# Another order of stages in a hybrid encoder step: the sample tile first, no stage behind its producer, no empty slots

## The reference

```
h = x + 0.5 * rms(SwiGLU_1(rms(x)))                    F1: 1024 -> 2 x 2816 -> 1024
z = rms(h) @ w_in                                      IP: 5376 columns: q | k | v | r,k,v,lora | gates
A = differential attention (4 heads, two softmax maps, rotary; prompt: block-causal, sample: 1024 cached keys + 16 own)
B = RWKV-7 mixing (8 heads of 64; each row's input is mixed with the row before it; a 64x64 state runs on)
m = sigmoid(gA) * (A @ w_o_att) + sigmoid(gB) * (B @ w_o_rwkv)
h = h + rms(m @ w_out)                                 OP
y = h + 0.5 * rms(SwiGLU_2(rms(h)))                    F2
```

## Time and profile before

| | us |
|---|---|
| median of 3 runs (3283.29 to 3289.14) | 3287.9 |
| time of the profiled execution | 3277.8 |
| its span | 3275.9 |
| PE busy | 3052.7 (93%) |
| DVE, ACT, POOL busy | 1732.7, 1263.5, 474.0 |
| mean granted TensorE clock | 0.968 of full |

### The profile page before, as it was taken

The page is one execution under the profiler, slowest core; times in us unless marked ns, Lnnn a source line. Parts: engine busy times, 40 slices in busy tenths (PEclk is TensorE's granted clock), DMA queues, the critical chain, the costliest instruction groups (busy, mean ns, idle before and its releaser), DMA issues.

```text
span 3275.9 us, 58322 instructions
## 1 busy us (share of the span) xinstructions
PE 3052.7 (93%) x23880; PEld 2701.3 (82%) x23880; DVE 1732.7 (53%) x2956; ACT 1263.5 (39%) x2494; POOL 474.0 (14%) x609
## 2 busy tenths in 40 slices
PE   7999999999999999989999899899889999996997
PEld 7998999789898877977779779787678788886996
DVE  4456445445556455376465555566555553454454
ACT  4334334344433343344344334333333332343432
POOL 0000000003022040220220310411411401200000
PEclk9999999999999999999999999999989998998998
DMA  5445444556334364564454433445644633463443
GB/s 153 126 127 175 133 129 142 188 177 205 94 118 136 117 217 140 154 204 153 137 156 130 141 103 95 140 152 195 200 140 141 194 124 111 144 210 126 126 129 112
DMA packets 499814, 482.78 MB, mean 147 GB/s; under 512 B 28563, under 2 KB 401708, under 8 KB 499534
## 3 DMA queue, kind: packets, MB, share of 16 engines
q1 hardware_dynamic: 472846, 389.16, 38.2%
q0 software_dynamic: 26704, 89.91, 8.6%
HBM read 431.77 MB, written 48.18 MB: 147 GB/s over the span
## 4 chain that ended last, share of the span: by engine, by line
PE 81%; DVE 7%; DMA 4%; issue 3%; ACT 2%; POOL 1%; SPq 0%; DVEq 0%; ACTq 0%; POOLq 0%
PE ps L252 41%; PE ps L262 25%; PE ps L978 4%; PE ps L1661 1%; DVE wlo L217 1%; PE ps L1677 1%; PE ps L1703 1%; DMA att<-out_dram 1%; DVE yb L884 1%; DMA att<-in_cache_att_v_dram 1%; ACT gB L826 1%; PE ps L983 1%; PE ps L970 1%; PE ps L1714 1%; DVE xnlo L539 1%
## 5 line engine op out<-in xcount | busy, mean ns | idle before, releaser
L217 DVE TENSOR_TENSOR wlo<-raw,whi 128x512 fp32r<-128x512 f32 x1140 | 823.8, 725 | 945.9 <-ACT whi L209 943.8
L209 ACT ACTIVATE whi<-raw 128x512 fp32r<-128x512 f32 x1140 | 712.8, 629 | 741.7 <-PE ps L252 389.0
L252 PE MATMUL ps<-xnhi,whi 128*128 128x384 f32 x2688 | 931.7, 347 | 18.9 <-issue 9.0
L252 PE MATMUL ps<-xnhi,wlo 128*128 128x384 f32 x2688 | 906.6, 337 | 0.0
L252 PE MATMUL ps<-xnlo,whi 128*128 128x384 f32 x2688 | 906.3, 337 | 0.0
L252 PEld LDWEIGHTS ps<-xnhi,whi 128*128 128x128 f32 x2688 | 510.4, 190 | 47.2 <-issue 27.7
L252 PEld LDWEIGHTS ps<-xnlo,whi 128*128 128x128 f32 x2688 | 510.8, 190 | 2.0 <-issue 1.7
L252 PEld LDWEIGHTS ps<-xnhi,wlo 128*128 128x128 f32 x2688 | 510.0, 190 | 0.0
L262 PE MATMUL ps<-whi,hidhi 128*128 128x512 f32 x936 | 384.7, 411 | 8.9 <-DVE yb L585 4.1
L262 PE MATMUL ps<-wlo,hidhi 128*128 128x512 f32 x936 | 369.3, 395 | 0.0
L262 PE MATMUL ps<-whi,hidlo 128*128 128x512 f32 x936 | 369.1, 394 | 0.0
(11 more groups left out here) (294 smaller groups left out, 3252.1 us busy)
## 6 DMA issues: line engine op xcount, KB each, us to landing
raw<-in_ffn_w_in_dram SPq DMA_DIRECT2D x528, 256.0 KB, 2.9
raw<-in_ffn_w_out_dram SPq DMA_DIRECT2D x264, 256.0 KB, 2.6
raw<-in_w_in_dram SPq DMA_DIRECT2D x252, 256.0 KB, 2.8
xt<-h_scratch SPq DMA_DIRECT2D x36, 512.0 KB, 5.5
att<-in_cache_att_k_dram POOLq DMA_DIRECT2D x32, 512.0 KB, 5.7
att<-in_cache_att_v_dram POOLq DMA_DIRECT2D x32, 512.0 KB, 4.4
rw<-zr_scratch POOLq DMA_DIRECT2D x51, 256.0 KB, 7.1
raw<-in_w_out_dram SPq DMA_DIRECT2D x48, 256.0 KB, 2.9
```

The costliest lines, as they stand in the source:

```text
L209: act.activation(B["whi"][:, slot], B["raw"][:, slot], ACT.Copy).then_inc(E["whi"], 1)
L217: dve.tensor_tensor(B["wlo"][:, slot], B["raw"][:, slot], B["whi"][:, slot].bitcast(F32), ALU.subtract).then_inc(E["wlo"], 1)
L252: ins = pe.matmul(ps[:, bank, 0:BT], B["w" + wt][:, n % RING, i * P:(i + 1) * P], x(xt, i), start=first and i == 0 and (wt, xt) == passes[ ...
```

## The change

1. `TILE_OF = [8, 0, 1, ...]`: the sample is tile 0 of block 0, the prompt tiles follow. The blocks are now {sample, 0, 1}, {2, 3, 4}, {5, 6, 7}. In att, the sample comes first; the prompt heads then have 2, 3 and 3 tiles.
2. `STAGES` is new: IP 1 stands before F1 2, and F2 1 behind OP 2, so that no F2 follows its OP. `depends` and `gaps` go: 1140 slots, and every stage is entered from within the last 8 slabs of the one in front, IP's successor too.
3. IP has a new order: 4 gate pieces, attention's q and k, r, lora, k, v, 12 gate pieces, attention's v. rw may start 4 slots behind its v (slab 52), att of block 0 ten slots before the end of IP.
4. POOL issues the loads of a head at the LD of the head in front of it (`load_head`); those of a block's first head still at its own LD.
5. Dues are shared out anew over rw and att of all blocks, and lie 19 slots before an OP.

```
-STAGES = [("F1", 0), ("F1", 1), ("IP", 0), ("F1", 2), ("IP", 1), ("OP", 0), ("IP", 2), ("F2", 0), ("OP", 1), ("F2", 1), ("OP", 2), ("F2", 2)]
+STAGES = [("F1", 0), ("F1", 1), ("IP", 0), ("IP", 1), ("F1", 2), ("OP", 0), ("IP", 2), ("F2", 0), ("OP", 1), ("OP", 2), ("F2", 1), ("F2", 2)]
+TILE_OF = [8, 0, 1, 2, 3, 4, 5, 6, 7]
-DEP_GAP, IP_GAP = 14, 2
-XP = ["r", "k", "v", "l", "aq", "ak", "av"]
+XP = ["aq", "ak", "r", "l", "k", "v", "av"]
+IP_ORDER = [("g", u) for u in range(4)] + [("x", pi) for pi in range(6)] + [("g", u) for u in range(4, 16)] + [("x", 6)]
+IP_RW, IP_LAST = 52, 76
 def inside(k):
-    return STAGES[k][0] != "IP" and k + 1 < len(STAGES) and not depends(k + 1)
+    return k + 1 < len(STAGES)
...
@@ dense_pe, IP @@
+                    if i == len(XP) - 1:
+                        enter(k + 1, s)
...
@@ dense_act, enter @@
-        if kk == 0 and k > 0:
+        if k and STAGES[k - 1][0] == "IP":
+            act.wait_ge(E["used"], FIRST[k - 1] + IP_LAST + kk + 1)
+        elif k and kk == 0:
             act.wait_ge(E["used"], FIRST[k - 1] + LAST_OF_X[STAGES[k - 1][0]])
...
@@ att_pool @@
+    def load_head(blk, h, head):
+        buf, c0, nt = head % 2, TILE0[blk] * P, TILES_IN[blk]
+        nk = TILE0[blk] + nt
+        if head >= 2:
+            pool.wait_ge(E["att_ot"], NB + head - 1)
+        pool.dma_start(V["kT"][buf][:, 0:nk * P], t["kT"][h * P:(h + 1) * P, 0:nk * P]).then_inc(E["att_ld%d" % buf], 16)
+        pool.dma_start(V["q"][buf][:, 0:nt * P], t["qT"][h * P:(h + 1) * P, c0:c0 + nt * P]).then_inc(E["att_ld%d" % buf], 16)
+        pool.dma_start(V["v"][buf][:, 0:nk], t["new_v_prompt"].rearrange("(k p) c -> p k c", p=P)[:, 0:nk, h * P:(h + 1) * P]).then_inc(E["att_ld%d" % buf], 16)
...
+            if h == 0:
+                load_head(blk, 0, heads)
+            if h + 1 < HEADS:
+                load_head(blk, h + 1, heads + 1)
...
@@ timetable @@
+            ready = start[STAGES.index(("IP", blk))] + (IP_RW if name == "rw" else NSLAB["IP"]) + 4 - (14 if (name, blk) == ("att", 0) else 0)
+            due = start[STAGES.index(("OP", blk))] - 8 - PRE_STEPS - 6
+            begin = max(ready, reached)
+            last = start[STAGES.index(("OP", 2))] - 8 - PRE_STEPS - 6
+            due = min(due, int(begin + (last - begin) * total[blk] / sum(total[blk:])))
```

More of the change, by code:

```diff
@@ L136, in buffers, with tile_rows @@
     return B
-def tile_rows(t, what, tile):
+def tile_rows(t, what, at):
+    tile = TILE_OF[at]
     if tile < SEQ // P:
@@ L336, in dense_pe @@
                         for tl in range(NT):
[L337 to L345, removed]
+                            bk.give(names[tl], E["zcopy"], z_number(ii, i, tl) + 1)
                     n += 1
@@ L710, in dense_sp @@
                 yield
-        for _ in range(gaps(k)):
-            yield
 def gates_sp(sp, B, E, t):
@@ L986, in rw_pe @@
     for p in range(PAIRS):
-        kd = int(p == PAIRS - 1)
+        kd = int(p == 0)
+        tile = TILE_OF[p]
         yield "LD"
@@ L2011, in att_pool @@
         yield "X"
+        if b == 0:
+            for i in range(6):
+                pool.wait_ge(E["zst%d" % i], 16 * z_stores(i, len(XP) * NT))
+            new_values(0)
         yield "M"
@@ new lines, in att_pool @@
+    pool.wait_ge(E["att_st0"], 16)
+    for n, (blk, h, tile) in enumerate(UNITS):
+        first, last_of_head = head_units(n)
+        if first:
+            if h == 0:
+                for i in TWO:
+                    pool.wait_ge(E["qst%d" % i], 16 * 3 * (blk + 1))
+                for i in range(6):
+                    pool.wait_ge(E["zst%d" % i], 16 * z_stores(i, (blk + 1) * len(XP) * NT))
+            if h == 0:
+                load_head(blk, 0, heads)
+            if h + 1 < HEADS:
+                load_head(blk, h + 1, heads + 1)
+            yield "LD"
+        for c in chunks_of(tile):
+            yield "S"
+        yield "X"
+        yield "T"
+        pool.wait_ge(E["att_sq"], n + 1)
+        if n:
+            pool.wait_ge(E["att_ov"], n)
+        else:
+            pool.wait_ge(E["z_ov"], NB)
+        pool.tensor_scalar(st[:, 22:23], st[:, 20:21], 1.0 / P, EPS, ALU.mult, ALU.add).then_inc(E["att_ms"], 1)
+        pool.wait_ge(E["att_ms"], n + 1)
+        pool.tensor_tensor(st[:, 22:23], st[:, 22:23], halfc, ALU.pow).then_inc(E["att_rs"], 1)
+        yield "V"
+        yield "W"
+        if last_of_head:
+            heads += 1
+            nt = TILES_IN[blk]
+            c0 = (TILE0[blk] + 1) * P
+            pool.wait_ge(E["att_oe"], NB + heads)
+            pool.dma_start(t["attT"][h * P:(h + 1) * P, c0:c0 + nt * P], V["oT"][:, 0:nt * P]).then_inc(E["att_st%d" % blk], 16)
+            yield "O"
@@ L2136, in timetable @@
         if what == "post":
-            norm += [start[k + 1] - gaps(k) * (k + 1 < len(STAGES) and depends(k + 1)) + i for i in range(POST_STEPS)]
+            norm += [start[k + 1] + i for i in range(POST_STEPS)]
         elif k:
-            enter = start[k] - (8 if inside(k - 1) else 2)
-            norm += [enter - PRE_STEPS + i for i in range(PRE_STEPS)]
+            norm += [start[k] - 8 - PRE_STEPS + i for i in range(PRE_STEPS)]
     assert norm == sorted(norm) and len(set(norm)) == len(norm), norm
@@ L2156, in timetable @@
             at, prev = 0.0, begin - 1
-            for s in steps:
-                at += cost.get(s, 1)
+            for s in steps[blk]:
+                at += COST[name].get(s, 1)
                 prev = max(prev + 1, int(begin + at * scale))
                 side[name].append(prev)
-            assert prev <= start[op] - 8, (blk, name, prev, due)
-            reached[name] = prev + 1
-    return start, slab_of, norm, side
+            assert prev <= start[STAGES.index(("OP", blk))] - 8, (blk, name, begin, prev, due, scale)
@@ L2172, in weave @@
         for n in range(issued, FIRST[-1]):
-            at = slab_of.index(n) if n < ahead else slab_of.index(n - ahead)
-            events[-1 if n < ahead else at].append("weights")
+            events[max(-1, n - ahead)].append("weights")
     if queue:
```

592 lines of the change are left out of this document (280 added, 312 removed).

## The result

| | before | after |
|---|---|---|
| median on the same chip, 4 runs each | 3285.6 us (3282.9 to 3289.1) | 3208.1 us (3206.3 to 3211.0) |
| profiled execution | 3277.8 us | 3211.0 us |
| its span | 3275.9 us | 3209.2 us |
| PE busy | 3052.7 us (93%) | 3049.1 us (95%) |
| span less PE busy | 223.2 us | 160.1 us |

The ratio is 0.9764, with a 95% interval of 0.9747 to 0.9781: 77 us faster. The forecast was 3222, with 3188 to 3281. The row of the half clock in the table is worked out from the trace: the stretches in which a clock record says 0.50, as far as PE was busy in them. With it the whole difference can be written as two terms. PE busy less half of that time is 2990.7 us before and 2989.8 after, the same work. So 66.7 us of span are 63.1 us of less idle time and 3.6 of less busy time, of which 2.7 is the clock.

A forecast was written before the change was run, and what follows sets the result against it. PE, busy 93% of the span, bounds the kernel, with its work unchanged. Savings of 111 us less 45 us of new costs give -66: span 3210, median 3222 us, range 3188 to 3281.

The forecast's parts named there:

- A: The 35.8 us gap between OP 2 and F2 2 goes; its transposes remain between slabs; 33 us saved.
- B: The 45.7 us gap between OP 1 and F2 1 goes; its rw and att steps move elsewhere; 29 us saved.
- C: Joints of IP: waits before OP 0 and for the first panel's buffer go, with half clock behind them; 24 us saved.
- D: Late loads of attention heads: issued one head earlier, most of 19.8 us of waits and half clock go; 25 us saved.
- E: More rw and att steps stand one slot behind the step they need; 24 us of new waits, bounds 5 and 60.
- F: New neighbours at OP 0, the sample's rw start and its cache loads add 11 us of waits, bounds 0 and 25.
- G: Half clock on PE behind the new waits, at half the rate of late head loads; 10 us, bounds 0 and 27.
- The other reading, small products alone: Small products on PE lower the clock without any hole, so the squeezed steps might run at 0.95; 26 us.
- R2: Rival: squeezing rw and att costs up to 62 us more; median 3263, between 3250 and 3281; chance 0.22.
- R5: Rival: squeezing rw and att is free; net -96 to -103, 3185 to 3192 us; chance 0.08.
- R4: Rival: part of the 35.8 us gap, say 25, returns inside OP 2; 3247 us; chance 0.04.
- R3: Rival: POOL is late at sample entries; six holes cancel the gain, nine give 3318 us; chance 0.10.

The follow-up runs named there:

- experiment 3: Changed kernel with F2 1 before OP 2 and both 14-slot gaps again, rw and att keeping slots 323 to 825: 3268.2 us, ratio 0.9961.
- experiment 1: Changed kernel with every head's loads issued at its own LD again: 3232.5 us, ratio 0.9852 to the kernel before.
- experiment 6: Changed kernel with F1 2 in front of IP 1 again, as before the change: 3229.0 us, ratio 0.9831.
- experiment 2: Changed kernel with F2 1 before OP 2 and both 14-slot gaps again, rw and att allowed in slots 324 to 971: 3229.3 us, ratio 0.9842.
- experiments 4 and 12: Changed kernel with T and V2 at twice their cost in the spreading of att, run twice: 3195.9 us (0.9747) and 3197.7 us (0.9736).
- experiment 8: Changed kernel with the sample's attention six slots earlier and T at twice its cost: 3212.3 us, ratio 0.9786.
- 7: Changed kernel with the sample's attention begun six slots earlier: 3230.2 us, ratio 0.984.
- 9: Changed kernel with the sample's attention begun six slots later: 3204.3 us, ratio 0.9752.
- The second execution: The changed kernel run once more as it is, unaltered, in a later set on one chip: 3210.8 us, ratio 0.9774.

## Why the prediction was right, and where its terms were off

*The total.* Forecast for the span: -66, to 3210. Measured between the profiled executions: -66.7, to 3209.2. That the two agree within 1 us is luck: the medians lie 77.5 us apart, and the 12 us by which before's runs lay above its profiled span, and which I added, were in good part a higher clock in that one execution (0.968 for a mean of 0.966). Against the medians the forecast is 11 us short.

*A and B, the gaps: right in the main.* Forecast 33 + 29 = 62. Both gaps vanish. I had named 3 us as the most that L274 would still wait; behind the start its longest wait is 3.1, at the end of IP 2. Putting two gaps back costs 61 to 65 us. The agreement with 62 is closer than it should be: the gaps of experiment 3 are both empty, so the rule of term A (length less 2.5) gives 67 for them. Term B, a gap with steps in it, was not undone as it stood.

*C, the joints: signs right, the size only partly tested.* The three waits are gone (0.2 us is left). Gate pieces first are worth 5 to 9 us of the 24. The 9.0 us in front of OP 0 are gone as well, but that part was not undone by itself.

*D, the heads: right.* Forecast 25; undoing it costs 26 to 29, and att<-out_dram ends 2.9 us of waits, under the 5 that I named.

*E and F, new waits: in their net effect 12 us less than forecast.* The waits and gap idle of A to D come to 31.2 + 23.0 + 16.6 + 15.7 (the last as experiment 1 measured it) = 86.5 us. 223.2 - 86.5 = 136.7 would be left, 160.1 are there: 23 us of new waits, where E and F had 35. But this 23 is a balance. It also holds what the rest of the change saved, such as the new place of IP 1 (17.3 us of idle time in experiment 6). The spacing alone costs 30 us or so of idle time by experiments 2 and 3, over the 24 of E. T, M, V1 and V2 together wait 35.4 us, within the 30 to 40 named. The rows of rw's lines sum to 27.2 us, a little over the 25 named. IP 1 and F1 2, the two densest stages, lose 60.0 us to idle time and half clock, and lost 28.1 before: 32 more, under the 50 that I had named as the sign of being wrong.

*G, half clock behind new waits: its reason was weak, its size can't be settled by one pair of profiles.* What goes with A to D at half clock was, by my terms, 7.7 + 6.4 + 8 + 2 = 24 us of loss. The measured change between the profiled executions is (123.9 - 118.6) / 2 = 2.7, so the new arrangement adds some 21, not 10. Between typical executions the clock gives back some 10 us more, as the section on the result has it, and then G is 10 to 12. In the profiles of experiments 2 and 3 the squeeze adds nothing at half clock (114.0 and 111.3). So G was not shown to be mis-sized, and not shown to be right. Two things in it were wrong. Half of the rate of D (8 lost behind 19.8) is 0.20, and 35 us of waits give 7 by it, not the 10 written. And "at half of that rate, since most new waits are short" doesn't hold as a reason: the windows above show waits of 2 to 3 us followed by 3.4 or 6.8 us at half clock, as much loss per us of wait as behind the long ones, or more, and others of the same length followed by none. The other reading, small products alone, is visible in one stretch of 17.1 us (8.6 lost); most of the rest stands behind holes. By the rule cited in the prediction ("TensorE: Matmul & The Clock Gate", Part 1, in the Trainium skill) it is activity that releases the throttle. The trace agrees only in the sense in which the prediction took it: the stretch from 875.9 has small products alone. In the profile's sense of busy it doesn't agree, since PE is busy there for 17.10 of 17.10 us and is granted 0.50.

*The rivals.* R2 (squeeze dear, 62 more): no, though experiment 2 came out in the branch named after it; the squeeze cost some 30 us, 39 at most. R5 (free): no. R4 (gap back in OP 2): no, OP 2 takes 74.8 us. R3 (POOL late for the sample) needed six holes to take the gain. Three of over 5 us are there, each with half clock behind it: 8.0 us for the first keys in IP 0, 5.6 and 6.3 us for values in IP 1 and F1 2. Only the first of them is POOL coming late. In the other two POOL was waiting itself. Its timeline for that of 6.3 us, and then that of PE:

```profile
1182.21 0.54 POOL L1512 DMA_DIRECT2D rw<-zr_scratch  x1
1184.00 0.71 POOL L1953 DMA_DIRECT2D att<-in_cache_att_v_dram  x1 [1.25 <-PE ps L1693]
```

```profile
1183.02 1.08 PE L1693 MATMUL ps<-att 128*32 128x128 f32 x32
1186.34 0.64 PE L1693 MATMUL ps<-att 128*32 128x128 f32 x16
1193.30 1.66 PE L1693 MATMUL ps<-att 128*32 128x128 f32 x24 [6.32 <-DMA att<-in_cache_att_v_dram]
```

POOL stands idle until V1 (1183.02) has freed a buffer, issues the load at 1184.00, and V2, one slot behind V1, can use it only at 1193.30. A whole transfer must fit between V1 and V2, and this one was slow besides: 9.3 us, where the median of these loads is 4.6, behind the eleven loads of rw that POOL issued from 1176.91 to 1182.21 and with the DMA engines full:

```profile
1184.00:1193.30 9.30, 2.98 (x32) 2.43 (x28) 1.02 (x2) 0.24 (x1) 1.44 (x2) 0.82 1.05 367
```

The hole of 5.6 us has the same picture. With V2 two slots behind, in experiments 4 and 12, the row falls to 3.4 us; in experiment 8, where only T got more room, it still has 13.4. The place counts too: with the sample six slots earlier or later and no more room, in 7 and 9, the row has 7.2 and 10.5. Taking rw's loads away from there was not tried. The prediction had named this distance in F, with 3 us, and in E as a close step at 0.23 us, with up to 0.49; the row has 18.0 us in six waits, 3.0 each.

*Not in the sum at all:* that IP 1 ahead of F1 2 is worth 19 to 22 us (experiment 6). I had counted slots after the change as given and charged the squeeze, but not asked what the squeeze would be with the old order of these two.

*Not tested by itself:* the sample as the first tile, the new shares of the dues, and the joint in front of OP 0. They are part of every variant.

## What to carry to other kernels

Split the span first into idle time of the bounding engine and its busy time at half clock: with the work unchanged the idle time and half of the half-clock time explain every variant here within 4 us, and show in which of them a forecast is off. Look at the granted clock of several executions before a difference of 10 us is read from one pair of profiles. A stage that must wait for its producer's last store, load and scale costs a gap (36 us here when it is empty), of which side steps fill only a part (17.6 of 39.5 us in experiment 2); another stage between them removes it, and the price is that the side steps stand closer (some 30 us here). When side steps share a fixed number of slots, spacing one kind moves most of its waits to others (27 of 34 us), so look for the steps whose wait is a whole transfer or the first load of a string, and try their place in both directions: six slots earlier cost 22 to 25 us, six later gained 6.5, hardly clear of the noise, and with the spacing 31, clearly.

## What the runs showed of the hardware that was not expected

- A hole of 2 to 3 us on PE can be followed by 3.4 or 6.8 us at half clock with PE busy (the pairs of windows above), and whether it is differs between two executions of the same program: one wait of 2.61 us was followed by 6.8 us at 0.50 in the one and by full clock in the other. On the whole the changed kernel loses 59.3 us at half clock (118.6 / 2) beside 130.4 us of idle time between PE's first and last instruction.
- PE can fall to half clock without any hole: 171 small matmuls, 17.10 of 17.10 us busy, at 0.50, behind 139 in 9.9 us at 1.00. The second execution has 206 in 20.5 us at the same place.
- Executions of one kernel differ by their granted clock: the one before by 18 us between 0.963 and 0.969. A profile shows one of them.
- A load of 512 KB that lands in 4.6 us in the median took 9.3 us behind eleven loads of another string, with a DMA share of 1.05.
- PE busy, less half of its time at half clock, is 2986.0 to 2993.3 us in all 14 profiles, whatever the order of stages and steps.
